# One stage instead of two: attention over selected keys and key compression join the selected and window attention, and the selection of keys is spread over 20 of 24 steps

## The reference, cut to what matters

```python
# branch b: an index score chooses 128 keys per query
rel = relu(einsum('bqhd,bkd->bqhk', q_idx, k_idx));  score = einsum('bqh,bqhk->bqk', w_idx, rel)
score = where(kpos <= qpos, score, -inf);  _, sel = top_k(score, 128)
o_b = masked_softmax(q_b . k_b[sel] / 8) @ v_b[sel]                     # 4 heads of 64
# branch c: three attentions with four query heads on one key head each
kc, vc = compress(k_cmp), compress(v_cmp)      # blocks of 32 tokens, 2048 -> 128, gelu, 128 -> 64
o_c = g0 * attend(q_c, kc, vc) + g1 * attend(q_c, k_sel, v_sel) + g2 * attend(q_c, k_win, v_win)
merged = sigmoid(g_merge[0]) * (o_a @ up0) + sigmoid(g_merge[1]) * (o_b @ up1) + sigmoid(g_merge[2]) * (o_c @ up2)
```

## Time and profile before

| what | us |
|---|---|
| median of three runs | 1696.13 |
| profiled execution, its own time | 1698.2 |
| its span | 1696.4 |
| TensorE matmul busy | 1598.5 (94%) |
| VectorE busy | 796.9 (47%) |
| ScalarE busy | 645.3 (38%) |
| GpSimd busy | 245.5 (14%) |

### The profile page before, as it was taken

The page is one execution under the profiler, slowest core; times in us unless marked ns, Lnnn a source line. Parts: engine busy times, 40 slices in busy tenths (PEclk is TensorE's granted clock), DMA queues, the critical chain, the costliest instruction groups (busy, mean ns, idle before and its releaser), DMA issues. The chain is left out here.

```text
span 1696.4 us, 20739 instructions
## 1 busy us (share of the span) xinstructions
PE 1598.5 (94%) x7924; PEld 1293.0 (76%) x7924; DVE 796.9 (47%) x1582; ACT 645.3 (38%) x1306; POOL 245.5 (14%) x148
## 2 busy tenths in 40 slices
PE   7999999899799999899999999789989999999998
PEld 6888777677687877777878778668767788887886
DVE  4222388746724344446534467646553433333223
ACT  4222455542513156624235634463243422222112
POOL 0000022367200011120012242112100000000000
PEclk9999999999899999999999999889995999999999
DMA  5332211111232321023421221012220223322322
GB/s 200 99 100 99 76 51 52 36 63 38 88 99 75 100 75 38 26 88 105 147 77 60 87 75 63 26 51 88 90 72 13 87 89 98 100 99 88 100 91 83
DMA packets 38338, 135.25 MB, mean 80 GB/s; under 512 B 4640, under 2 KB 5024, under 8 KB 38112
## 3 DMA queue, kind: packets, MB, share of 16 engines
q1 hardware_dynamic: 34400, 125.32, 22.6%
q10 hardware_dynamic: 3840, 8.61, 1.5%
HBM read 128.02 MB, written 2.10 MB: 77 GB/s over the span
## 5 line engine op out<-in xcount | busy, mean ns | idle before, releaser
L210 ACT ACTIVATE cut_hi<-raw 128x1024 fp32r<-128x1024 f32 x228 | 241.6, 1060 | 644.8 <-PE ps L227 631.3
L227 PE MATMUL ps<-h_hi,cut_hi 128*128 128x512 f32 (+1 forms) x1120 | 453.9, 405 | 5.1 <-DVE h_lo L425 3.2
L215 DVE TENSOR_TENSOR cut_lo<-raw,cut_hi 128x1024 fp32r<-128x1024 f32 x172 | 212.9, 1238 | 496.3 <-ACT cut_hi L210 494.5
L229 PE MATMUL ps<-h_hi,cut_lo 128*128 128x512 f32 (+1 forms) x1120 | 437.3, 390 | 0.0
L228 PE MATMUL ps<-h_lo,cut_hi 128*128 128x512 f32 (+1 forms) x1120 | 436.9, 390 | 0.0
L227 PEld LDWEIGHTS ps<-h_hi,cut_hi 128*128 128x128 f32 x1120 | 211.7, 189 | 76.9 <-issue 29.4
L229 PEld LDWEIGHTS ps<-h_hi,cut_lo 128*128 128x128 f32 x1120 | 211.5, 189 | 45.0
L228 PEld LDWEIGHTS ps<-h_lo,cut_hi 128*128 128x128 f32 x1120 | 212.2, 189 | 37.8
L215 POOL TENSOR_TENSOR cut_lo<-raw,cut_hi 128x1024 fp32r<-128x1024 f32 x56 | 133.9, 2392 | 682.3 <-ACT cut_hi L210 682.3
L227 PE MATMUL ps<-cut_hi,h_hi 128*128 128x512 f32 (+1 forms) x368 | 142.2, 386 | 7.8 <-DVE cut_lo L215 6.4
L229 PE MATMUL ps<-cut_hi,h_lo 128*128 128x512 f32 (+1 forms) x368 | 141.5, 385 | 0.0
(11 more groups left out here) (304 smaller groups left out, 2076.1 us busy)
## 6 DMA issues: line engine op xcount, KB each, us to landing
raw<-weights SPq DMA_DIRECT2D x228, 512.0 KB, 3.3
scr<-scr ACTq DMA_DIRECT2D x34, 64.0 KB, 3.6
x<-x_in SPq DMA_DIRECT2D x4, 512.0 KB, 6.3
x<-x_in ACTq DMA_DIRECT2D x1, 2048.0 KB, 7.5
out<-x SPq DMA_DIRECT2D x4, 512.0 KB, 2.6
consts<-tables ACTq DMA_DIRECT2D x1, 1732.0 KB, 7.8
arena<-arena ACTq DMA_DIRECT2D x12, 128.0 KB, 2.4
arena<-mem_in SPq DMA_DIRECT2D x1, 1024.0 KB, 4.9
```

The source lines that it names most:

```text
L210: act.activation(cut_hi[:, u % CUT, :], raw[:, u % RAW, :], ACT.Copy).then_inc(hi_ready, 1)
L215: eng.tensor_tensor(cut_lo[:, u % CUT, :], raw[:, u % RAW, :], cut_hi[:, u % CUT, :].bitcast(F32), ALU.subtract).then_inc(lo_ready, 1)
L227: a = pe.matmul(out, left[0], right[0], start=start, stop=False)
L229: return a, pe.matmul(out, left[1], right[0], start=False, stop=stop)
```

## The change

The 8 units of "dsa" are appended to the 16 of "swa", and one call of `attend_pairs` runs all 24. The fill is a new part, `GatesThenBlocks`: the gates' 13 remaining units (104 turns), 8 turns without work, then the compression's 32 turns, 144 in all, 6 a step instead of 7. ScalarE's turn that ends the gates and rounds the blocks, and VectorE's that makes block_lo, are due at turn 107, in step 17. The selection's 51 turns are dealt over 20 steps instead of 16, that is 2 or 3 a step. From unit 18 on VectorE waits for the mask of the tile before it takes a maximum.

```diff
-                        return (min(step + 1, n) * lead.turns // n - min(step, n) * lead.turns // n) if lead else 0
+                        if not lead:
+                            return 0
+                        return min(step + 1, lead.span) * lead.turns // lead.span - min(step, lead.span) * lead.turns // lead.span
...
+                            if "mask_ready" in u:
+                                dve.wait_ge(*u["mask_ready"])
...
-            turns = 3 * P // 8 + 3
+            turns, span = 3 * P // 8 + 3, 20
...
-        attend_pairs("swa", units, S, fill=fill_m3, lead=Selection())
-
         class Compression(Part):
...
             def act(self, act):
+                act.wait_ge(fill_m3.done, fill_m3.n)
+                act.wait_ge(cm_blocks, 2)
                 act.activation(block_hi[:, :, :], blocks, ACT.Copy).then_inc(cm_hi, 1)
+                yield
...
-            def prepare(self, dve):
+            def dve(self, dve):
                 dve.memset(vc_diag, 0.0).then_inc(cm_diag, 1)
                 dve.wait_ge(cm_hi, 1)
                 dve.tensor_tensor(block_lo[:, :, :], blocks, block_hi[:, :, :].bitcast(F32), ALU.subtract)\
                    .then_inc(cm_lo, 1)
-
-            def dve(self, dve):
-                for _ in range(4):
+                for _ in range(5):
                     yield
...
+        class GatesThenBlocks(Part):
...
+            n = cuts = fill_m3.n + Compression.n
+            u0, blocks, rest = fill_m3.u0, Compression(), 8
+            pe_turns, span = KD * (fill_m3.n - 1) + rest + Compression.pe_turns, None
+            starts = (*range(0, KD * (fill_m3.n - 1), KD), KD * (fill_m3.n - 1) + 3,
+                      *range(KD * (fill_m3.n - 1) + rest, KD * (fill_m3.n - 1) + rest + Compression.pe_turns, KD))
+
+            def pe(self, pe):
+                yield from fill_m3.pe(pe)
+                for _ in range(self.rest):
+                    yield
+                yield from self.blocks.pe(pe)
...
+            def act(self, act):
+                gate_turns = fill_m3.act(act)
+                for _ in range(fill_m3.n):
+                    next(gate_turns)
+                    yield
+                for _ in gate_turns:
+                    pass
+                yield from self.blocks.act(act)
...
+                if t:
+                    units[-1]["mask_ready"] = (ix_sel, t)
+        attend_pairs("swa", units, S, fill=GatesThenBlocks(), lead=Selection())
```

More of the change, by code:

```diff
@@ L2236, in build @@
                                       gate=tv[:, t, 453 + j + 3 * h:457 + j + 3 * h:3], add=j == 1))
-        attend_pairs("swa", units, S, fill=fill_m3, lead=Selection())
         class Compression(Part):
             n = cuts = 4
-            pe_turns, starts = 32, range(0, 32, 8)
+            pe_turns = 32
             u0 = START["cmp"]
@@ L2297, in dve @@
                     dve.tensor_copy(vc_diag[rows_h, h * 64:(h + 1) * 64], ps[rows_h, 7, 0:64]).then_inc(cm_out, 1)
[L2299 to L2303, removed]
+        class GatesThenBlocks(Part):
[17 more added lines that the diff above has]
+                yield from self.blocks.act(act)
+            def dve(self, dve):
+                for _ in range(fill_m3.n):
+                    yield
+                yield from self.blocks.dve(dve)
         for t in range(NT):
@@ L2310, in build @@
                                   out=o_abc[:, t, 256 + h * 64:256 + (h + 2) * 64]))
-        attend_pairs("dsa", units, S, fill=Compression())
+                if t:
+                    units[-1]["mask_ready"] = (ix_sel, t)
+        attend_pairs("swa", units, S, fill=GatesThenBlocks(), lead=Selection())
         cs_names = ["cs_scored", "cs_chain", "cs_shifted", "cs_exp", "cs_prob", "cs_turned", "cs_pT", "cs_valued",
```

## The result

| what | before | after |
|---|---|---|
| median of ten executions each, us | 1685.53 (1679.83 to 1698.05) | 1679.70 (1674.23 to 1684.55) |
| ratio of means | | 0.9943, interval 0.9916 to 0.9971 |
| profiled execution, us | 1698.2 | 1675.65 |
| its span | 1696.4 | 1673.8 |
| TensorE matmul busy | 1598.5 (94%) | 1582.8 (95%) |

The account below looks back on a forecast made before the run. TensorE and VectorE were taken as limiting different stages, with TensorE starving at the seam and at half clock after it. -12.6 + 7.9 = -4.7 us gave 1691 us; inner range 1687 to 1695 (0.52), outer 1675 to 1700.

Parts of the forecast that it names:

- A: Merged stage: VectorE runs far enough ahead, no wait in steps 17 to 20; 1683.5 us, chance 0.08.
- B: Merged stage: VectorE already late from step 13, everything given back; 1696 us, no change, chance 0.14.
- C: Memory attention behind the stage: it runs at full clock instead of 0.50; 1676 us, chance 0.20.
- What is taken away (12.6): Seam between the two stages: output wait 4.8, drain 3.4, block_lo wait 2.0, half clock 2.4; 12.6 us saved.
- What it adds (7.9): Steps 17 to 19: TensorE's steps shrink while VectorE has rounds and block_lo left; 3.3 + 2.5 + 2.1 = 7.9 us.
- Its first term: Step 17: TensorE waits 3.3 us for VectorE's output of unit 14, behind block_lo and two rounds.
- The other two terms: Steps 18 and 19: half clock on TensorE, 2.5 us, and a further wait for VectorE, 2.1 us.
- VectorE's 12.6: VectorE's work in steps 18 and 19: six rounds, two outputs, two maxima and the mask, 12.6 us.
- about 2.5 more: Steps 18 and 19: TensorE at half clock after its wait in step 17, about 2.5 us more.
- waits 2.1 more: Steps 18 and 19: TensorE, ahead by 1.6 us, waits 2.1 us more for VectorE.
- Two smaller edits cost nothing: Mask wait at steps 18 to 23 and weight-unit starts every 8 turns in steps of 6: no cost, bounds -2 to +4.
- D: Steps 18 to 26: clock falls and stays low to the merged stage's end; 21 us more, 1712 us, chance 0.06.

Follow-up runs that it names:

- the merge alone: Changed kernel with the selection dealt over 16 steps instead of 20, run on two chips: medians 1669.74 and 1672.63 us, ratios to the kernel before 0.992 and 0.9895.
- before_pad: Kernel before the change with 22 more matmuls (5.0 us, result overwritten) on TensorE ahead of the stage: ratio 1.0017 to the kernel before.
- busy_wait: Changed kernel with three unread matmuls in the empty turns where TensorE would wait: median 1677.01 us, ratio 0.9927 to the kernel before.
- span17: Changed kernel with the selection's turns dealt over 17 steps instead of 20: median 1673.41 us, ratio 0.9911 to the kernel before.
- the padded one: Changed kernel with 22 more matmuls (5.0 us, result overwritten) on TensorE ahead of the stage: ratio 0.9981 to the kernel before.
- again_2: Changed kernel, unaltered, run once more on another chip for comparison: median 1678.6 us, ratio 0.9924 to the kernel before.

## Why the prediction was right, and where not

The forecast itself held: the stage shrank by 5.1 us in the two profiled executions (5.1 to 6.5 over three traces of the changed kernel, with the start's 1.7 taken off), where the sum was 4.7. The median is 1679.7, 11 under the forecast of 1691 and 7 under its inner range; 1691 was set on the median of the three executions shown, two of which were long ones (1696.13 and 1698.05), and ten of the same kernel have 1685.5. From there the forecast of -4.7 gives 1680.8. The outer range held the median because it was drawn to take in rivals A, B and C as well.

*What is taken away (12.6).* Right. The runs give 161.6 for the stage before and 149.2 to 149.6 for the merge alone, so 12.0 to 12.4. Part of this is luck of the trace: against before_pad, whose stage took 164.96, it would be 15.3 to 15.8. The Trainium skill, "Perfetto Trace Analysis", section "Optimization Strategy", says that interleaving regimes with different bounds may help; with 16 or 17 steps for the selection this kernel gets all that it has to give, and in the form of the change about half. Rival A was no rival of the merge, only of the spread.

*What it adds (7.9).* The sum was somewhat too large: the runs give 156.5 - 149.3 = 7.2, and 5.9 and 6.4 in the two other traces of the changed kernel. Its first term was met: 3.3 forecast, 3.33 measured in all three, from the order of VectorE's instructions and their durations in the trace before. That it is met so closely has some luck in it: from the scores of step 17 TensorE was ready at 5.55 us and not 5.2, and went on at 8.88 and not 8.5, two misses that cancel. The other two terms are one quantity, and in the prediction's own sum they are: VectorE's 12.6 less TensorE's 3.3 + 3.1 and its lead of 1.6 gives 4.6, whatever part of it is half clock and whatever part a wait. How it was shared out was off: "about 2.5 more" for half clock assumes some 5 us of it and the traces have 10.2 and 6.8, and in place of "waits 2.1 more" there is no wait for L1088 and none to 0.6 for L1091. The runs bear out the exchange: with TensorE at half speed its own steps fill the time of VectorE's rounds, and with TensorE kept at full speed (busy_wait) the time comes back as a wait. What was wrong in size is the 12.6, by a miscount: steps 18 and 19 have five rounds, not six. Less one round of 1.52 it is 11.1 (the trace has 10.7, from the end of the output at 1088.96 to the end of that of unit 16 at 1099.62), the wait becomes 0.6 and the additions 6.4, well inside the 5.9 to 7.2 measured. That VectorE's work in those steps sets the time of the last mask was right.

*"Two smaller edits cost nothing".* Right: TensorE's waits for ScalarE's copies are 3.0 in the changed stage, 3.3 in the stage before and 3.7 in that without rounds, and no wait for a mask appears.

*Rivals.* B (all given back) falls: there is no wait for VectorE ahead of step 17, not even with three turns in each step. D falls: the clock is back at 1.00 within 14 us in every trace of the merged stage. C has a share in the result. The first comparison and the three groups give 73 executions of the kernel before, of which 21 are some 13 us above the rest; of 29 of the changed kernel none is. In the first comparison it was 4 of 10, at 13 us each 5.2 of the 9.4 between the means (1688.4 and 1679.0), and the stage gives some 5; over all 73 it would be 13 x 21 / 73 = 3.7. That the long executions are a matter of the clock stands on record: in the three groups their mean granted clock is 0.964 to 0.969, in all others of the kernel before 0.972 to 0.978, and 1683 x 0.976 / 0.968 = 1697. That the low clock lies in the memory attention is inferred: the only trace of a long one has 37.3 us there, and twelve traces of others, of all kernels, have 24.2 to 26.7. Why the changed kernel shows none stays open. It can hardly be chance, if executions are independent of each other: 29 in a row at 52 of 73 each is 0.00005. But it is not the merge by itself, since 8 of 52 executions of its variants lie some 10 to 14 above the rest, 3 of 9 of span17 and one of 12 of the padded one (1693.57, at a mean clock of 0.967) among them. Nor does the distance from the start decide it alone, by the trace of before_pad. The Trainium skill, "TensorE: Matmul & The Clock Gate", section "What's actually happening", says of a kernel's start that the number of half-rate matmuls differs between runs of one kernel. The traces show such a difference in the middle of one: 10.2, 6.8 and 6.8 us of the lower clock behind the wait in three traces of the changed kernel, and 24.6, 24.7 and 26.5 us for its memory attention.

## What to carry to other kernels

When a stage that starves one engine is merged with one that starves the other, deal the surplus engine's work so that it ends before the filler of the bound engine runs out; here that choice (16 or 17 steps, not 20) was worth 6 of 12 us, and an even load per step was the wrong aim. On an engine that works its list in order, as VectorE did here, an instruction that waits for another engine holds the ready work behind it and everyone who waits for that work (here 2.37 us of idle VectorE, and 2.1 to 3.5 us of the stage): put it behind, not ahead. And compare two traces by the stretch between the same two instructions before explaining the difference of their spans; here 12.7 of 22.6 us lay in code that both kernels share.

## What the runs showed that was not expected

- Low clock beside a second limit was hidden there: TensorE's stretched work replaced waits for VectorE, and the last mask came 129.6 us into the stage with the clock low beside the rounds (again_2) and with it low mostly behind them (busy_wait). Behind the rounds it was paid: 28.9 us to the end instead of 27.2.
- In the memory attention, TensorE was busy 36.6 of 40 us at 0.50 in one execution and ran at 0.84 to 1.00 in twelve others. Sixteen us of small matmuls (64 to 256 columns) without a pause, from 1272 to 1288, did not bring the clock back there, while in the merged stage it was back within 14 us.
- A wait of 3.33 us and one of 1.72 us, both among short matmuls, were each followed by low clock; the seam with its waits of 4.84 and 1.96 had 13.6 us of it in one trace and 20.5 in another. The wait of 1.8 us ahead of the stage had some 3.4 us of it behind it in six traces and none in five. The length of the wait alone does not tell the cost.
